# Attention: the score and output products of a pair's two heads issued alternately, each in its half of the array

## The reference

```python
def band_attend(q, k, v, bias, valid):
    s = jnp.einsum("bqhd,bkhd->bhqk", q, k).astype(jnp.float32) * ATT_SCALE + bias
    s = jnp.where(valid, s, jnp.finfo(jnp.float32).min)
    p = jax.nn.softmax(s, axis=-1).astype(v.dtype)
    return jnp.einsum("bhqk,bkhd->bqhd", p, v)
...
    start = ci * CHUNK
    qc = lax.dynamic_slice_in_dim(q, start, CHUNK, axis=1)
    kc = lax.dynamic_slice_in_dim(kp, start, BAND, axis=1)
    vc = lax.dynamic_slice_in_dim(vp, start, BAND, axis=1)
    return band_attend(qc, kc, vc, bias, (start + k_off) >= 0)
```

## Time and profile before

| | |
|---|---|
| median of 3 runs | 5020.41 us |
| lowest and highest | 5019.88, 5023.28 us |
| span of the profiled execution | 5024.5 us |
| PE busy in it | 4518.3 us (90%) |
| DVE, ACT, POOL busy | 2050.3, 1480.1, 574.0 us |
| mean granted TensorE clock | 0.935 |

### The profile page before, as it was taken

The page is one execution under the profiler, slowest core; times in us unless marked ns, Lnnn a source line. Parts: engine busy times, 40 slices in busy tenths (PEclk is TensorE's granted clock), DMA queues, the critical chain, the costliest instruction groups (busy, mean ns, idle before and its releaser), DMA issues. The chain is left out here.

```text
span 5024.5 us, 69286 instructions
## 1 busy us (share of the span) xinstructions
PE 4518.3 (90%) x25724; PEld 4165.4 (83%) x25724; DVE 2050.3 (41%) x3699; ACT 1480.1 (29%) x2543; POOL 574.0 (11%) x547
## 2 busy tenths in 40 slices
PE   6799899999999999865488878997999999999998
PEld 3599898999999999764366657997999999999997
DVE  3400344444444444443245544333435444353442
ACT  2311222222222222211134333123334344343432
POOL 1210222232222223221000000000000000000000
PEclk9899999999999999977569878998999999999999
DMA  6422111111111111000400004333434434344342
GB/s 223 149 72 69 43 37 38 47 36 36 44 40 36 36 47 37 24 10 7 147 9 8 8 29 156 109 105 102 129 111 118 126 109 137 110 122 123 109 127 81
DMA packets 595632, 390.45 MB, mean 78 GB/s; under 512 B 99313, under 2 KB 585353, under 8 KB 594449
## 3 DMA queue, kind: packets, MB, share of 16 engines
q1 hardware_dynamic: 528336, 309.63, 21.8%
q10 hardware_dynamic: 67136, 78.63, 4.4%
HBM read 306.86 MB, written 81.34 MB: 77 GB/s over the span
## 5 line engine op out<-in xcount | busy, mean ns | idle before, releaser
L522 PE MATMUL proj_ps<-h_hi,w_hi 128*128 128x416 f32 x1680 | 601.2, 358 | 14.8 <-POOL w_lo L507 14.8
L522 PE MATMUL proj_ps<-h_hi,w_lo 128*128 128x416 f32 x1680 | 611.6, 364 | 0.0
L522 PE MATMUL proj_ps<-h_lo,w_hi 128*128 128x416 f32 x1680 | 603.1, 359 | 0.0
L2008 DVE TENSOR_TENSOR ff_lo<-ff_raw,ff_hi 128x1024 fp32r<-128x1024 f32 x320 | 391.5, 1224 | 449.8 <-ACT ff_hi L2004 449.5
L1609 PE MATMUL ff_ps<-h_hi,ff_hi 128*128 128x416 f32 x1280 | 462.9, 362 | 25.5 <-DVE ff_lo L2008 23.9
L2004 ACT ACTIVATE ff_hi<-ff_raw 128x1024 fp32r<-128x1024 f32 x320 | 337.8, 1056 | 454.2 <-PE ff_ps L1609 431.3
L1609 PE MATMUL ff_ps<-hidden_hi,ff_hi 128*128 128x416 f32 x1280 | 459.5, 359 | 3.6 <-DVE ff_lo L2008 3.6
L1609 PE MATMUL ff_ps<-h_hi,ff_lo 128*128 128x416 f32 x1280 | 452.4, 353 | 0.0
L1609 PE MATMUL ff_ps<-hidden_hi,ff_lo 128*128 128x416 f32 x1280 | 451.5, 353 | 0.0
L1609 PE MATMUL ff_ps<-h_lo,ff_hi 128*128 128x416 f32 x1280 | 448.3, 350 | 0.0
L1609 PE MATMUL ff_ps<-hidden_lo,ff_hi 128*128 128x416 f32 x1280 | 447.3, 349 | 0.0
(11 more groups left out here) (288 smaller groups left out, 7666.1 us busy)
## 6 DMA issues: line engine op xcount, KB each, us to landing
ff_raw<-in_w_ff SPq DMA_DIRECT2D x320, 512.0 KB, 4.0
keep_proj<-proj_out ACTq DMA_DIRECT2D x210, 208.0 KB, 1.9
ada_w<-in_w_ada SPq DMA_DIRECT2D x24, 1024.0 KB, 5.8
w_raw<-in_w_in SPq DMA_DIRECT2D x42, 512.0 KB, 4.4
gates<-keep_proj SPq DMA_DIRECT2D x80, 208.0 KB, 2.4
rows_in<-keep_proj SPq DMA_DIRECT2D x32, 448.0 KB, 5.3
x_then_x<-keep_xT SPq DMA_DIRECT2D x40, 208.0 KB, 2.5
keep_x2T<-x_then_x ACTq DMA_DIRECT2D x40, 208.0 KB, 1.9
```

The costliest lines, as they stand in the source:

```text
L522: mm = pe.matmul(self.ps[u][:, 0:BW], w[:, par, kk, :], a[:, kk, cols], start=(kk == 0 and j == 0), stop=(kk == KD - 1 and j == 2))
L2008: w.lo_s.done(dve.tensor_tensor(w.wlo[:, s % 2], w.raw[:, s % 4], w.whi[:, s % 2].bitcast(F32), ALU.subtract), s)
```

## The change

Four things are altered, all in class `Heads`. The step list `self.order` of VectorE and ScalarE now has, behind t of an odd head, the s of the next two heads together, and n of a head always behind t of the head before it. TensorE's list `pe` goes by pairs: both T, then both S of the next pair, then both Y. `scores` takes a pair and issues its products alternately, 512 columns of the even head, 512 of the odd, then 128 of each. Y takes only the 64 columns of V of its own head, writes the 64 partitions of the result that are read, and is issued alternately for the two heads, piece by piece. The waits are the same, for the steps in their new places; both Y of a pair wait for t of the odd head. The number of products and their columns of keys stay; an output product has 64 stationary columns in place of 128.

```diff
         order = [("s", 0), ("s", 1), ("n", 0)]
         for h in range(NH):
-            order += [("t", h)] + [("n", h + 1)] * (h + 1 < NH) + [("s", h + 2)] * (h + 2 < NH)
+            order += [("t", h)] + [("s", h + 1), ("s", h + 2)] * (h % 2 and h + 2 < NH) + [("n", h + 1)] * (h + 1 < NH)
...
         pe = [("s", 0), ("s", 1)]
-        for h in range(NH):
-            pe += [("t", h)] + [("s", h + 2)] * (h + 2 < NH) + [("y", h)]
+        for h in range(0, NH, 2):
+            pe += [("t", h), ("t", h + 1)] + [("s", h + 2), ("s", h + 3)] * (h + 2 < NH) + [("y", h), ("y", h + 1)]
...
-        def scores(h):
-            if h == 0:
+        def scores(h0):
+            if h0 == 0:
                 self.keys_s.wait(pe, "K", turn)
                 self.queries_s.wait(pe, "q", turn)
-
-            v.wait(pe, ("s", h - 2), turn) if h >= 2 else v.wait(pe, ("s", h + NH - 2), turn - 1)
-            rows = slice(64 * (h % 2), 64 * (h % 2) + 64)
-            for x0, x1 in ((c0, min(c1, 512)), (512, c1)):
-                if x1 > x0:
+            for h in (h0, h0 + 1):
+                v.wait(pe, ("s", h - 2), turn) if h >= 2 else v.wait(pe, ("s", h + NH - 2), turn - 1)
+            parts = [x for x in ((c0, min(c1, 512)), (512, c1)) if x[1] > x[0]]
+            for x0, x1 in parts:
+                for h in (h0, h0 + 1):
+                    rows = slice(64 * (h % 2), 64 * (h % 2) + 64)
                     mm = pe.matmul(self.ps_s[h % 2][0:nq, x0:x1], self.q[rows, h // 2, 0:nq], self.K[rows, h // 2, x0:x1],
                                    start=True, stop=True)
-            p.done(mm, ("s", h))
-        scores(0)
-        scores(1)
-        for h in range(NH):
+                    if x1 == c1:
+                        p.done(mm, ("s", h))
+
+        def turn_probs(h):
             v.wait(pe, ("n", h), turn)
...
-            if h + 2 < NH:
-                scores(h + 2)
-            v.wait(pe, ("t", h), turn)
-            a.wait(pe, ("t", h), turn)
-            if h == 0:
+        scores(0)
+        for h0 in range(0, NH, 2):
+            turn_probs(h0)
+            turn_probs(h0 + 1)
+            if h0 + 2 < NH:
+                scores(h0 + 2)
+            v.wait(pe, ("t", h0 + 1), turn)
+            a.wait(pe, ("t", h0 + 1), turn)
+            if h0 == 0:
                 v.wait(pe, "V", turn)
                 a.wait(pe, "yT1", turn - 1)
             tl = self.tiles(c0, c1)
             for i, (c, n) in enumerate(tl):
-                mm = pe.matmul(self.ps_y[h % 2][:, h // 2, 0:nq], self.Vw[0:n, c // P, (h // 2) * P:(h // 2 + 1) * P], self.eT[0:n, h % 2, c:c + nq],
-                               start=(i == 0), stop=(i == len(tl) - 1))
-            p.done(mm, ("y", h))
+                for h in (h0, h0 + 1):
+                    rows = slice(64 * (h % 2), 64 * (h % 2) + 64)
+                    mm = pe.matmul(self.ps_y[h % 2][rows, h // 2, 0:nq], self.Vw[0:n, c // P, h * HD:(h + 1) * HD], self.eT[0:n, h % 2, c:c + nq],
+                                   start=(i == 0), stop=(i == len(tl) - 1))
+                    if i == len(tl) - 1:
+                        p.done(mm, ("y", h))
```

## The result

The changed kernel takes 5070.81 us (median; 5065.03 to 5074.22) where the kernel before takes 5020.28 us beside it: a ratio of 1.0096, 95% interval 1.0081 to 1.011. It is slower by some 50 us, and the span of its profiled execution is 5071.9 us. The forecast was 5084 with a range from 5038 to 5150.

A forecast was written before the change was run, and what follows sets the result against it. TensorE bounds the full tiles, but after the change the chain through TensorE, VectorE and ScalarE would. 5020.4 + 69 (twelve full tiles) - 5 (short tiles), sample 0, gives about 5084 us, range 5038 to 5150.

The forecast's parts named there:

- a chain through three engines: In a pair of heads, TensorE's 2.39 us less work hides under VectorE and ScalarE steps; the pair gets 0.90 longer.
- The pair at the upper clock: Two heads in a full tile's middle at 2.4 GHz: 7.18 us forecast against 6.28 before.
- s to the next T: From a head's row maximum with bias (VectorE) to the next pair's first probability transposes (TensorE): 2.87 us.
- The keys' copy: VectorE's copy of the next tile's keys delays head 6's scaling by the sum, and its transposes: 1.09 us per tile.
- S and Y in halves: A pair's score products in row halves take 1.28 us, its output products in column halves 1.11, both side by side.
- rival B: Output products of two heads do not run side by side: full tiles +8.6 us, about 5118 (5095 to 5155); chance 0.17.
- The clock: Full tiles lie midway between all 2.4 GHz (32.0 us) and all 1.2 GHz (43.0): 37.5, +69 us over twelve.
- Short tiles and sample: Four short tiles before the full ones: -5 us; the sample tile, one of seventeen: 0, within 3 either way.
- C: Clock stays at the upper level throughout the stage: full tiles +3, short tiles up to -22, about 5008; chance 0.04.
- D: Lower clock throughout the full tiles: +134 us, about 5150; chance 0.08.
- E: Clock falls only in about a fifth of the full tiles' time: about 5045 us; chance 0.16.
- A's: The forecast itself: clock lower in a third to two thirds of full tiles' time, about 5084 (5060 to 5106); chance 0.52.

The follow-up runs named there:

- best: Changed kernel with both score products between the two transposes, row maxima before the odd copy, both copies before both exponentials, next keys' copy later: 4938.76 us.
- y128_new_order: Changed kernel with output products on 128 columns again, issued head after head: 5087.25 us, ratio 1.0126 to the kernel before.
- y64_old_order: Kernel before, its order kept, with each head's output product on its own 64 columns: 5018.62 us, ratio 0.9987.
- no_alternation: Changed kernel with a pair's score and output products issued head after head, each still in its own half: 5050.71 us, ratio 1.0056 to the kernel before.
- fill_gaps: Changed kernel with unread products added, four between a pair's two transposes and five behind its output products: 5029.31 us, ratio 1.0012 to the kernel before.

## Why the prediction was right, and where it was off

**The bound and the chain.** Right. The forecast was that TensorE's saving lies under a chain through three engines, and the 84 new waits of T for n are that chain. The pair at the upper clock was put at 7.18 us and is 6.81. T to odd T was 2.17 and is 2.11, S to s 1.39 and is 1.39. The mis-sized step is s to the next T, taken as 2.87 from a tile's start and 2.62 in the middle of a tile. So two of the signs came out low: the pair is under the 7 us at the upper clock (9.10 at the lower), and the wait ahead of the even T is 1.42 and not about 1.9.

**The keys' copy.** Right: 1.09 us a tile were forecast, 1.08 (2.50 less 1.42) are in the trace. That taking it away gives 19 us, where the waits fall by only some 7, was not.

**S and Y in halves.** Right, both: the S pair takes 1.28 (2749.31 to 2750.59), and the Y pair 1.24 where it stands ahead of T (2718.09 to 2719.33 in `best`), where 1.11 was taken. (The 1.11 stands between two weight loads; between products one head's Y took 1.22 before, so the two of a pair together take what one took.) So rival B fell: it needed Y records one behind the other. y128_new_order, which has them so, costs 11 us more in the full tiles (446.87 - 435.64) where B said 34. But its granted clock is 0.78 and not 0.73, so this is not B's price at one clock: a pair of its Y takes 4.43 us at the lower clock (2768.02 to 2772.45), and the chain from s to T leaves room for only 2.73 of them (2750.59 to 2753.32 in the changed kernel).

**The rule that speaks for B.** The Trainium skill ("TensorE: Matmul & The Clock Gate", section The mechanism) has, in its list of what overlaps, a weight load overlap a running product only when their row groups differ. The Y loads of both heads take all 128 rows, and twenty of them with their products fit into 1.31 us, which is as long as ten take in y64_old_order. So here the trace goes against it.

**The clock.** That the clock would fall for part of each tile was right. How large a part, half, was a choice without a row; the granted clock of 0.73 is 54% of the time at the lower level ((1 - 0.73) / 0.5). That the choice came so near is luck: no_alternation, with the same chain and the same pair of 6.82 us at the upper clock, has 0.86, which is 28%. The tile was put at 37.5 us and is 36.3 (435.64 / 12): +55.7 in place of +69. Both ends of the sum were mis-sized. The start of a tile at the upper clock is

```profile
2733.61 1.35 PE L1470 MATMUL scores_ps<-k_window,q_tile 64*128 64x512 f32 x8
2738.18 0.76 PE L1480 MATMUL probs_ps<-identity,probs 128*128 128x128 f32 x5 [3.21 <-ACT probs L1442]
```

so 4.57 us to the first T; with three pairs at 6.81, 1.08, 2.11, 1.35 to Y and 1.24 for Y the tile takes 30.8 us, where 32.0 stood. At the lower clock it is 5.42 to the first T (2876.24 to 2881.66), three pairs at 9.10 where 9.76 was taken, 1.08, 2.67, 1.92 to Y (2985.82 to 2987.74) and 2.33 for Y: 40.7 us, where 43.0 stood. The pairs make most of it at both ends, by s to the next T. The measured 36.3 lies 56% of the way from 30.8 to 40.7, which agrees with the 54% of the time. Both whole tiles are worked out from rows; no tile ran wholly at either clock.

**Short tiles and sample.** Forecast -5 and 0 within 3, found -2.2 and -4.8. The sample was put at 0 without working, and what that left out is its narrow Y: at the lower clock and 32 queries, y64_old_order shows it alone to be worth 4.1 us. In the short tiles the narrow Y gives nothing: 104.39 us against 100.84 in the old order, and 98.65 against 93.84 (y128_new_order) in the new one, there at a granted clock of 0.55 against 0.74.

**The rivals.** C, the clock staying up, did not happen. fill_gaps brings the clock to 0.96 by force, and its ratio of 1.0012 is no gain even then, where C said 5008; its added products take time of their own, so it bounds C from above only. By the 30.8 us above, the full tiles would take about 10 us less than before if the clock stayed up, so it is C's condition that did not hold, and not its price that was shown wrong. D (lower clock throughout) and E (a fifth of the time) are out by the 0.73. That alternation itself does nothing holds for S and falls for Y; that the time would then be A's fell too, since it was 20 us less.

**What stays open.** Why head after head keeps the clock at 0.86, the wide Y at 0.78 and the alternated halves at 0.73 in the same order. The idle place ahead of T is 0.71, 0.24 and 1.42 us in them, so its length alone does not rank them, and neither does TensorE's busy share (66%, 72%, 65%).

## What to carry to other kernels

Before an engine's work is made shorter, look at what stands in its gaps: here the S between two T was the cover of two other engines' steps, and the same halves lost 1.0% without it and won 0.8% with it (1.6% with the keys' copy and two more steps moved). Where the chain through other engines is the bound, shorter products on TensorE only make its idle places longer, and these can cost as much through the granted clock as through the waits (here some 32 and 24 us, an estimate from rows); products that nothing reads show in one run how much the clock has in it. A one-shot copy that is queued on a shared engine goes behind the step that somebody waits for, and even there it can hold the next one back (0.45 us here).

## What the runs showed of the hardware that was not expected

- Float32 products with 64 stationary columns each, in the two column halves with all 128 rows, run side by side: 20 records in 1.31 us, against 2.50 for 20 records of 128 columns. One head alone gets nothing from it (10 records in 1.31; 1.24 us until the next T, against 1.22 with 128 columns).
- For the whole of this overlap Y must be issued alternately (head after head the pair takes 2.02 us, so a part is left); S in the row halves needs no alternation (1.35 and 1.36).
- More TensorE work made a kernel 42 us faster (fill_gaps), and a longer Y 20 us (no_alternation), both with a higher granted clock.
- The clock was not ranked by TensorE's busy share of the stretch: 65% and 0.73 (after), 66% and 0.86 (no_alternation), 66% and 0.92 (best), 72% and 0.78 (y128_new_order), 85% and 0.90 (before). The busy share itself grows where the clock is low: the 20 records of a narrow Y pair take 1.31 us at the upper clock and 2.40 at the lower.
